# Last two mixers: where the memory queries' norms are computed, and how the masked heads' norms sum their squares

## The reference

```python
for l in range(DEPTH):
    h = rms_norm(x, norm_g[l])
    q_a, k_a, v_a, q_h, f_h, i_h, q_m, z = split(h @ w_in[l])
    qa = partial_rope(rms_norm(q_a, moba_q_norm[l]), positions)      # 8 masked heads of 64
    ka = partial_rope(rms_norm(k_a, moba_k_norm[l]), positions)
    o_a = moba_attention(qa, ka, va)                                 # 256 tokens: causal attention
    o_h = rms_norm(hgrn2_chunkwise(q_h, f_h, i_h, lb), hgrn_o_norm[l])
    km = rms_norm(k_m, mem_k_norm[l])                                # keys of the memory
    qm = rms_norm(q_m, mem_q_norm[l])                                # 4 memory heads of 128
    o_m = memory_attention(qm, km, vm)
    x = x + (concatenate([o_a, o_h, o_m]) * silu(z)) @ w_out[l]
```

## Time and profile before

| | |
|---|---|
| time, median of three runs | 1533.81 us |
| the profiled execution's own time | 1533.24 us |
| its span | 1531.3 us |
| PE busy | 1495.4 us (98%) |
| DVE busy | 1170.6 us (76%) |
| ACT busy | 763.8 us (50%) |
| POOL busy | 100.0 us (7%) |

### The profile page before, as it was taken

How to read it: one execution, slowest core, us unless ns; L and a number is a source line. 1 busy time by engine, 2 the same in 40 slices (tenths; PEclk the granted TensorE clock), 3 DMA queues, 4 the chain that set the end, 5 groups by cost and what they waited for, 6 DMA issues and landing times.

```text
span 1531.3 us, 23925 instructions
## 1 busy us (share of the span) xinstructions
PE 1495.4 (98%) x9958; PEld 1343.6 (88%) x9958; DVE 1170.6 (76%) x1392; ACT 763.8 (50%) x937; POOL 100.0 (7%) x70
## 2 busy tenths in 40 slices
PE   8999999999999999999999999999999989999988
PEld 6888899989888888888998888888999869999967
DVE  7878768757887778877677788777779676589774
ACT  5434456535433463334555544345565675555673
POOL 2000010011000010000100100001213001103000
PEclk9999999999999999999999999999999999999999
DMA  8655535214655546555433465555444314544302
GB/s 271 216 193 191 168 139 192 83 56 150 220 189 192 191 165 208 182 189 192 164 140 111 157 222 183 195 180 179 149 169 162 106 36 176 207 141 163 110 29 83
DMA packets 51888, 246.76 MB, mean 161 GB/s; under 512 B 4619, under 2 KB 5771, under 8 KB 27718
## 3 DMA queue, kind: packets, MB, share of 16 engines
q1 hardware_dynamic: 50662, 238.29, 44.7%
q0 software_dynamic: 1120, 6.96, 1.2%
HBM read 244.18 MB, written 1.05 MB: 160 GB/s over the span
## 4 chain that ended last, share of the span: by engine, by line
PE 82%; DVE 8%; ACT 5%; issue 2%; POOL 0%; DVEq 0%; ACTq 0%
PE ps L1166 20%; PE ps L1168 10%; PE ps L1089 10%; PE ps L1091 10%; PE ps L1090 10%; PE ps L1219 9%; PE ps L1220 4%; PE ps L1383 4%; PE ps L1531 1%; ACT w_hi L1638 1%; DVE w_lo L1964 1%; ACT work L1851 1%; PE ps L1520 1%; DVE act_two L2072 1%; PE ps L1499 1%
## 5 line engine op out<-in xcount | busy, mean ns | idle before, releaser
L1638 ACT ACTIVATE w_hi<-raw 128x2048 fp32r<-128x2048 f32 x184 | 351.4, 1914 | 382.7 <-PE ps L1168 267.0
L1964 DVE TENSOR_TENSOR w_lo<-raw,w_hi 128x2048 fp32r<-128x2048 f32 x177 | 405.1, 2291 | 135.2 <-ACT w_hi L1638 132.9
L1166 PE MATMUL ps<-act_two,w_hi 128*128 128x512 f32 x1408 | 444.7, 397 | 2.6 <-DVE xn L1973 1.3
L1168 PEld LDWEIGHTS ps<-act_two,w_lo 128*128 128x128 f32 x1408 | 265.3, 188 | 63.1
L1089 PE MATMUL ps<-act_two,w_hi 128*128 128x256 f32 x1088 | 318.8, 293 | 1.0 <-DVE w_lo L1958 0.9
L1091 PE MATMUL ps<-act_two,w_lo 128*128 128x256 f32 x1088 | 307.7, 283 | 0.0
L1090 PE MATMUL ps<-act_two,w_hi 128*128 128x256 f32 x1088 | 307.7, 283 | 0.0
L1168 PE MATMUL ps<-act_two,w_lo 128*128 128x256 f32 x1408 | 277.4, 278 | 0.0
L1166 PEld LDWEIGHTS ps<-act_two,w_hi 128*128 128x128 f32 x1408 | 215.3, 189 | 5.3 <-DVE xn L1973 1.7
L1089 PEld LDWEIGHTS ps<-act_two,w_hi 128*128 128x128 f32 x1088 | 208.6, 192 | 5.8 <-issue 5.1
L1090 PEld LDWEIGHTS ps<-act_two,w_hi 128*128 128x128 f32 x1088 | 208.7, 192 | 4.2 <-issue 4.1
(11 more groups left out here) (294 smaller groups left out, 2065.0 us busy)
## 6 DMA issues: line engine op xcount, KB each, us to landing
raw<-panels SPq DMA_DIRECT2D x184, 1024.0 KB, 4.8
raw<-panels SPq DMA_DIRECT2D x80, 512.0 KB, 4.9
raw<-panels SPq DMA_DIRECT2D x8, 256.0 KB, 6.5
table<-tab POOLq DMA_DIRECT2D x1, 1472.0 KB, 8.9
table<-tab POOLq DMA_DIRECT2D x1, 1216.0 KB, 5.5
xn<-x_in SPq DMA_DIRECT2D x4, 256.0 KB, 4.3
work<-mem_in POOLq DMA_DIRECT2D x1, 1024.0 KB, 9.1
xn<-mem_in POOLq DMA_DIRECT2D x1, 1024.0 KB, 5.3
```

Source lines behind the costliest of these rows:

```text
L1166: pe.matmul(grid(ps[:, bank + half], 2), w[half][0], act_two[:, slots[c]], start=c == 0, stop=False)
L1168: ins = pe.matmul(ps[:, bank + half, 0:SEQ], w[half][1], act_hi[:, slots[c]], start=False, stop=c == DC - 1)
L1638: nc.scalar.activation(w_hi[:, s], raw[:, s], ACT.Copy).then_inc(panel_hi, 1)
L1964: tt(w_lo[:, s], raw[:, s], w_hi[:, s].bitcast(F32), ALU.subtract).then_inc(panel_lo, 1)
```

## The change

Two things are changed in both last mixers.

The norms of sq move from the heads' rounds to a chain of their own that begins at round n + 4: squares of (sq, 0) in round n + 4, its sum, `cn_rstd` and `cn_use` in round n + 5 together with the squares of (sq, 1), and the rest of (sq, 1) in round n + 6. In each of these rounds they stand ahead of the step of the same kind for ho. Their sums now go to banks 2 and 3, those of the rotations, and wait for `rope` of (mq, 1) and of (mk, 1).

The sums of mq and mk (four per layer) are no longer one product in full float32. ACT squares twice, once into a float32r buffer and once into the float32 buffer; POOL subtracts the first from the second (`cn_lo`), also into float32r; PE multiplies both parts by a float32r matrix of ones and adds them up in the same bank. The four buffers lie in `g_two`, which is free there.

`cn_sq` has a new wait for the sum of the norm two places earlier, whose squares lay in the same buffer.

```diff
+NORM_PARTS = [("pe", "cn_sum", 1), ("act", "cn_sq", 0), ("pool", "cn_lo", 0), ("act", "cn_rstd", 1), ("dve", "cn_use", 1)]
 NORM_COLS = [("pe", "cn_sum", 1), ("act", "cn_sq", 0), ("act", "cn_rstd", 1), ("dve", "cn_use", 1)]
...
-    out[0] += pair(0, ("pe", "scores")) + [("act", "evacuate", (f"in2_{l}", 19))] + norm("cn_sq", 0, 1) + norm("cn_sum", 0, 1)
+    out[0] += pair(0, ("pe", "scores")) + [("act", "evacuate", (f"in2_{l}", 19))]
     for p in range(4):
         a, b, c = 2 * p, 2 * p + 1, 2 * p + 2
         out[a] += pair(p, ("dve", "mask_max"), ("act", "exp"))
-        if p in (0, 1):
-            out[a] += norm("cn_rstd", p)
-        if p in (1, 2):
-            out[a] += norm("cn_use", p - 1)
...
     chains = [hgrn,
-              [[]] * n + rounds(NORM_COLS, qk + [(f"ho{l}", 0), (f"ho{l}", 1)]),
+              [[]] * (n + 4) + rounds(NORM_COLS, [(f"sq{l}", 0), (f"sq{l}", 1)]),
+              [[]] * n + rounds(NORM_PARTS, qk + [(f"ho{l}", 0), (f"ho{l}", 1)]),
...
+        ones_r = sb("ones_r", [P, 2, P], F32R)
...
+        sq_parts = [[g_two[:, 2 * i + j].rearrange("p a b -> p (a b)") for j in range(2)] for i in range(2)]
...
-                norms[f"sq{l}", g] = (qm[:, s2], ones, 1 / P, sm(f"sq{l}"), qm[:, s2], None, None, bank_of(f"in2_{l}", 18 + g), evac(f"in2_{l}", 16 + g))
+                norms[f"sq{l}", g] = (qm[:, s2], ones, 1 / P, sm(f"sq{l}"), qm[:, s2], None, None, 2 + g, evac(f"in2_{l}", 16 + g))
...
+            def cn_lo(unit):
+
+                i = norm_index[unit] % 2
+                pool.wait_ge(act_done, at("act", "cn_sq", unit))
+                hi, lo = sq_parts[i]
+                nc.gpsimd.tensor_tensor(lo, sq[i], hi.bitcast(F32), ALU.subtract).then_inc(pool_done, 1)
...
                 if unit[0][:2] == "sq":
-                    pe.wait_ge(act_done, at("act", "evacuate", "in2_" + unit[0][2], 18 + unit[1]))
+                    pe.wait_ge(dve_done, at("dve", "rope", (("mq", "mk")[unit[1]] + unit[0][2], 1)))
+                if unit in in_parts:
+                    pe.wait_ge(pool_done, at("pool", "cn_lo", unit))
+                    one, (hi, lo) = ones_r[:, int(unit[0][0] == "m")], sq_parts[norm_index[unit] % 2]
+                    pe.matmul(ps[:, bank], one, hi, start=True, stop=False)
+                    pe.matmul(ps[:, bank], one, lo, start=False, stop=True).then_inc(pe_done, 1)
+                    return
...
+                nc.scalar.activation(ones_r[:, 0], cst("ones"), ACT.Copy)
+                nc.scalar.activation(ones_r[:, 1], cst("ones64"), ACT.Copy)
...
+                if norm_index[unit] >= 2:
+                    act.wait_ge(pe_done, at("pe", "cn_sum", norm_list[norm_index[unit] - 2]))
...
+                if unit in in_parts:
+                    nc.scalar.activation(grid(sq_parts[norm_index[unit] % 2][0], 2), src, ACT.Square)
```

More of the change, by code:

```diff
@@ L412, in paired_heads @@
     pair = lambda p, *steps: [(e, k, ((f"moba{l}", h),)) for e, k in steps for h in (2 * p, 2 * p + 1)]
-    norm = lambda kind, *groups: [("pe" if kind == "cn_sum" else "dve" if kind == "cn_use" else "act", kind, ((f"sq{l}", g),)) for g in groups]
-    out[0] += pair(0, ("pe", "scores")) + [("act", "evacuate", (f"in2_{l}", 19))] + norm("cn_sq", 0, 1) + norm("cn_sum", 0, 1)
+    out[0] += pair(0, ("pe", "scores")) + [("act", "evacuate", (f"in2_{l}", 19))]
     for p in range(4):
@@ L444, in last_mixer @@
               [[]] * (h + 13) + [y_splits(l, 0), y_splits(l, 2)]]
+    chains[2] = [[x for x in r if x[1] != "cn_lo" or x[2][0] in qk] for r in chains[2]]
     if l == 0:
@@ L801, in build @@
                                       ("pe", "hgrn_out", l, g))
+        in_parts = [a[0] for e, k, a in ORDER if k == "cn_lo"]
         norm_list = [a[0] for e, k, a in ORDER if k == "cn_sum"]
@@ L1080, in store @@
                     pool.wait_ge(stored, 16 * TILES * 2)
-            steps("pool", {"load": load, "add": add, "zero": zero, "corner": corner, "k_level": k_level, "norm_x": norm_x, "store": store})
+            steps("pool", {"load": load, "add": add, "zero": zero, "corner": corner, "k_level": k_level, "norm_x": norm_x, "cn_lo": cn_lo, "store": store})
         @block.tensor
```

## The result

The changed kernel takes 1550.1 us (median of 4 runs, 1548.7 to 1551.7), the kernel before 1533.7 beside it: ratio 1.0110, 95% interval 1.0098 to 1.0122. A second session gave 1551.5 us and 1.0117 (1.0102 to 1.0131). It is slower, as forecast, by 16.4 to 17.9 us where the prediction had 12.2, and it lies at the upper edge of the predicted range in the first session and 1 us beyond it in the second. The predicted mechanism is there; the clock of TensorE came on top of it.

The account below looks back on a forecast made before the run. PE was taken to bound the kernel before the heads' rounds, DVE next; 6.7 us lost less 0.5 returned per layer, 6.1 as likely, twice 12.2, gave 1546.0 us. Its own range was 1542 to 1549, the stated range 1541 to 1550.5.

Parts of the forecast that it names:

- What bounds the kernel: Before the heads' rounds PE is full and DVE is next; within those rounds a chain of waits between engines.
- the seam: The passage from the stage where PE is full to the heads' rounds; layer 0 leaves PE at 1220.27.
- Part 1: Single products for sums of mq and mk: PE saves 1.6 us per layer, POOL's fourth subtraction costs DVE 1.0.
- my three quarters: Share of its overlap with POOL that DVE loses, read from the recurrence: 0.68 us lost in 0.89.
- Part 2: Norms of sq in front: PE waits 2.2 and 4.1 us for rotations, heads' first maximum 6.7 us late.
- Part 3: The heads' rounds get back 0.5 us per layer, 0.25 in each of two rounds; bounds 0 and 2.7.
- The sum: Per layer 6.7 - 0.5 = 6.2 us, 6.1 as likely; 12.2 us over both layers.
- a rival at 0.14: The clock falls as well, in PE's second stall: 3 us per layer, 1549 if once, 1552 in both; chance 0.14.
- the second wait: PE's stall of 4.1 us before the sum of (sq, 1), waiting for the rotation of (mk, 1) in bank 3.
- signs of being wrong altogether: No idle time of PE before the sums of sq, or a granted clock under 1.00.
- signs of being right: Two PE idle times, about 2 and 4 us; sums 4.2 us apart; first maximum 6 to 7 late; rounds 4.0.
- The rival of the queues alone: Bank waits cost nothing, only places in ACT's and DVE's order: 1.1 us per layer, 1536.0; chance 0.08.

Follow-up runs that it names:

- e2: Kernel before with only the single products for the sums of mq and mk, norms of sq left in the heads' rounds; 1531.9 us, ratio 0.9986.
- e7: Kernel before with only DVE's subtraction for the second half of the output's first panel moved behind the last masked head's division; 1532.9 us, ratio 0.9996.
- e11: Kernel before with single products alone, but the fourth sum of each layer, (mk, 1), kept in full float32; 1531.6 us, ratio 0.9982.
- e9: Changed kernel with own banks for the sums of sq and ho, plus 11 unread products behind the heads' first scores; 1536.9 us, ratio 1.0020.
- e14: Changed kernel with unread products in all three places where PE stands still, second session; 1545.6 us, ratio 1.0079.
- e4: Changed kernel with 8 and 16 unread products before the two sums of sq, waits for the rotations kept; 1547.7 us, ratio 1.0089.
- e1: Changed kernel with the sums of sq and ho in banks nothing else uses there, no sum waiting for a rotation; 1537.0 us, ratio 1.0025.
- e10: Changed kernel with unread products before both sums of sq and 9 more behind the heads' first scores, first session; 1547.3 us, ratio 1.0089.
- e3: Kernel before with only the norms of sq moved forward as in the changed kernel, all sums in full float32; 1552.8 us, ratio 1.0127.

## Why the prediction was right and wrong

**What bounds the kernel: right.** PE full before the seam, DVE next. e2 and e7 show both halves of that: PE's saving comes through until DVE, without a gap, takes 0.7 us of it, and a lighter DVE alone is worth nothing.

**Part 1: right.** The sums are 4.19 us apart. POOL's fourth subtraction cost DVE's rotation 0.96 us, predicted 1.0; e11 shows it by its absence. The rule that I weighed, in the Trainium skill, "SBUF — State Buffer", section "SBUF: two separate sides", has the one that began first block the other for its whole instruction. Here POOL ended at 1209.99, and DVE's operation, begun at 1208.90, at 1210.55, 0.56 us later, a little less than the 0.69 it takes alone. The trace lies midway: of 1.09 us of overlap DVE lost 0.96, by the rule all of it and by my three quarters 0.82. The rotation of (mq, 1) ends 17.92 us behind the first sum, predicted 18.07.

**Part 2: right at full clock.** The idle times are 1.94 us (predicted 2.2) and 4.20 where the clock held up to the second (predicted 4.1), 2.93 and 3.20 where it had fallen in the first. The first maximum is 6.8 us late with the clock full, in both layers and in three executions; predicted 6.7. e9 splits it: 5.2 us are the two waits, and 1.6 the place in the queues (2.5) less the gain of single products (0.9).

**Part 3: right in layer 0, too much in layer 1.** At full clock the heads' rounds give back 0.51 and 0.16 us, predicted 0.5 twice; why layer 1 gives less was not looked into. The rounds are 4.0 us each, as predicted (their first exponentials at 1236.35, 1240.36, 1244.36 and 1248.36 in e14). In the changed kernel itself the clock takes back two thirds of it in layer 0 and far more than all in layer 1: 27.82 and 30.41 us against 27.99 and 29.32.

**The sum** is therefore 12.98 us at full clock where 12.2 was predicted, and e14's ratio of 1.0079 is +12.1 us.

**The step that failed** is the one that gave the clock no term. The prediction weighed it as a rival at 0.14 and set against it that the clock at the end of the kernel fell only after 4.2 us without work and this gap is 4.1. That is one instance, read as a limit. The changed trace has the clock at half 0.5 us behind an idle time of 1.94 us, and e4 behind one of 1.64. The clock cost 5 to 6 us over both layers where the sum had 0. The Trainium skill, "TensorE: Matmul & The Clock Gate", in its part on the clock gate, says that the slow level is the default and that activity releases the fast one. e14, where idle time filled with useless products brings 1.00 back everywhere, agrees; that rule spoke for the rival. The rival's own price, 3 us per layer, was about right, its place too narrow: it named the second wait. The clock also fell in the first wait, and in a gap that I missed, because I asked of the two sums only what they cost the heads' rounds ("stand where ACT waits for DVE anyway") and not what they did for PE there. Without them PE stands still for up to 2.92 us (e1). Among its signs of being wrong altogether the prediction named a granted clock under 1.00, and that sign came, beside the two idle times and the spacing of 4.2 us that it had named as signs of being right; in the changed kernel itself the first maximum is 8.3 and 8.9 us late, outside its 6 to 7. That 1550.1 us still lies in the stated range does not speak for the sum, whose own range ended at 1549; the range had been drawn wider to take in the clock falling once.

**The rival of the queues alone** had 1.1 us per layer; e9, which takes the waits away and keeps the clock, has 1.11 and 1.46. That it comes so near is luck. The rival counted two `cn_use` and left out both DVE's wait for ACT (0.94 us) and the gain of single products (0.87), which nearly cancel. And it is not what the changed kernel does, since the rotations are late.

**The account**, both layers, from the stages: 1.7 us gained by single products (e2), 4.3 lost by the place in the queues (e9 less e2), 10.4 by the waits on the shared banks (e10 less e9), 5.2 by the clock (changed less e10), a loss of 18.15 in all. It takes the four as adding up; the small remainder between e2, e3 and the changed kernel shows that they do so only roughly.

## What to carry to other kernels

Before work is moved out of a waiting stage because it "only fills idle time" there, ask which engine it fills: PE's filler held the clock. Put a term for the clock on new idle time of PE, and don't set it to nothing because one row shows a longer gap through which the clock held: here it held through 1.94 us and fell within 0.91. And before a step is moved forward, look at who still uses its accumulation bank: two bank numbers and a wait took 14.7 of the 18.15 us away.

## What the runs showed of the hardware

The granted clock fell to half behind or within idle times of PE of 1.64, 1.94, 2.92, 2.93, 3.20 and 4.20 us, and in the heads' rounds also where the longest since its return was 0.91 (changed, second session, layer 1) or 0.92 us (changed, layer 0). It held at 1.00 through 1.94 us (changed, second session) and 1.31 us (e3) in both layers, and through all idle times of up to 0.98 us in the kernel before. The same gap of the same kernel lost the clock in one execution and not in the other. Where it fell, it stayed at half for 3.4 or 6.8 us though PE was busy again. A two-input operation of DVE (0.69 us) that began 0.21 us behind one of POOL took 1.65; POOL's, at 1.30, was not lengthened.
